# The mixer's input products of the second block from high and low parts, in three products instead of one four-byte product

## The reference

```python
def second_block(x, ...):
    for l in range(DEPTH):                                   # DEPTH = 2
        x = x + 0.5 * swiglu(rms_norm_2(x, norm_ffn1[l]), ffn1_in[l], ffn1_out[l])
        h = rms_norm_2(x, norm_mix[l])
        proj = h @ w_in[l]                                   # the mixer's input products
        p_rwkv, p_attn, p_gate = jnp.split(proj, [C_RWKV, C_RWKV + C_ATTN], axis=-1)
        o_a = rwkv7_mixer(p_rwkv, ...)                       # shift-mix, then a recurrent scan
        o_b = diff_attention(p_attn, ..., diff_lambda[l], ...)
        y = einsum(stack([o_a, o_b]), w_branch[l])
        x = x + sum(sigmoid(p_gate) * y) @ w_out[l]
        x = x + 0.5 * swiglu(rms_norm_2(x, norm_ffn2[l]), ffn2_in[l], ffn2_out[l])
```

## Time and profile before

| what | value |
|---|---|
| timed runs | 3978.73, 3982.89, 3984.99 us |
| the profiled execution | 3978.22 us, span 3976.5 us |
| busy share of the span | TensorE 86%, VectorE 39%, ScalarE 21%, GpSimd 15% |
| mean granted TensorE clock | 0.909 of full |
| second block | from 1953.7 us to the end |
| the mixer's input products | 2188.8 to 2282.1 us in layer 0, from 3195.2 us in layer 1 |

### The profile page before, as it was taken

How to read it: one execution, slowest core, us unless ns; L and a number is a source line. 1 busy time by engine, 2 the same in 40 slices (tenths; PEclk the granted TensorE clock), 3 DMA queues, 4 the chain that set the end, 5 groups by cost and what they waited for, 6 DMA issues and landing times.

```text
span 3976.5 us, 46296 instructions
## 1 busy us (share of the span) xinstructions
PE 3405.7 (86%) x18496; PEld 2349.6 (59%) x18496; DVE 1562.6 (39%) x2703; ACT 843.5 (21%) x1240; POOL 603.5 (15%) x556
## 2 busy tenths in 40 slices
PE   6878999993888799999199978787979997878799
PEld 3755334331566334333098658775978965868498
DVE  4433222224533222222454255543535425644354
ACT  1211111110130111111133232111324213111132
POOL 5402233331440233333000000000000000000000
PEclk8979999996878899999599988898999998889899
DMA  7646999995753899999554310003536422000442
GB/s 271 228 172 249 387 388 387 388 378 184 274 184 148 336 385 383 379 382 362 201 187 143 111 54 1 22 36 124 191 118 217 159 82 83 1 22 1 159 169 96
DMA packets 305420, 799.38 MB, mean 201 GB/s; under 512 B 57030, under 2 KB 155868, under 8 KB 251308
## 3 DMA queue, kind: packets, MB, share of 16 engines
q1 hardware_dynamic: 245804, 727.16, 48.4%
q0 software_dynamic: 58848, 67.05, 5.1%
q10 hardware_dynamic: 544, 2.10, 0.1%
HBM read 989.01 MB, written 53.48 MB: 262 GB/s over the span
## 4 chain that ended last, share of the span: by engine, by line
PE 41%; DVE 7%; ACT 1%; issue 1%; DMA 1%; SPq 0%; DVEq 0%
PE s_bank L1929 13%; PE s_bank L1967 6%; PE s_bank L1903 3%; PE s_bank L1916 3%; PE s_bank L2114 2%; PE s_bank L1994 2%; PE s_bank L2129 2%; PE s_bank L2225 2%; PE s_bank L2124 2%; PE s_bank L2235 1%; PE s_bank L2102 1%; DMA s_ringA<-in_ffn_in 1%; PE s_bank L2191 1%; PE s_bank L2025 0%; PE s_bank L2200 0%
## 5 line engine op out<-in xcount | busy, mean ns | idle before, releaser
L711 PE MATMUL f_bank<-f_ringA,f_arena 128*64 128x512 f32 x3072 | 689.8, 602 | 25.0 <-DMA f_ringA<-in_w_up,f_chosen 17.8
L711 PEld LDWEIGHTS f_bank<-f_ringA,f_arena 128*64 128x64 f32 x3072 | 216.5, 138 | 416.4 <-issue 415.2
L1929 PE MATMUL s_bank<-s_hT_high_parts,s_highA_parts 128*128 128x256 f32 x1408 | 402.1, 286 | 17.7 <-DVE s_hT_parts L2461 17.7
L1929 PE MATMUL s_bank<-s_hT_parts,s_highA_parts 128*128 128x256 f32 x1408 | 401.7, 285 | 0.0
L1929 PE MATMUL s_bank<-s_hT_high_parts,s_ringA_parts 128*128 128x256 f32 x1408 | 401.4, 285 | 0.0
L732 PE MATMUL f_bank<-f_ringB,f_arena 128*64 128x512 f32 x1536 | 346.1, 592 | 1.0 <-DVE f_arena L1475 1.0
L1012 ACT ACTIVATE f_arena<-f_bank 128x512 f32<-128x512 f32 (+1 forms) x362 | 202.0, 587 | 575.3 <-PE f_bank L692 174.1
L1467 DVE TENSOR_TENSOR f_arena<-f_arena,f_bank 128x256 f32<-128x256 f32 x96 | 58.6, 610 | 600.3 <-ACT f_arena L1090 600.3
L1929 PEld LDWEIGHTS s_bank<-s_hT_high_parts,s_highA_parts 128*128 128x128 f32 x1408 | 273.6, 194 | 20.4 <-issue 19.0
L1929 PEld LDWEIGHTS s_bank<-s_hT_parts,s_highA_parts 128*128 128x128 f32 x1408 | 273.6, 194 | 1.4
L1929 PEld LDWEIGHTS s_bank<-s_hT_high_parts,s_ringA_parts 128*128 128x128 f32 x1408 | 273.6, 194 | 0.0
(11 more groups left out here) (398 smaller groups left out, 5565.5 us busy)
## 6 DMA issues: line engine op xcount, KB each, us to landing
f_ringA<-in_w_gate SPq DMA_DIRECT2D x128, 1024.0 KB, 8.8
f_ringA<-in_w_up SPq DMA_DIRECT2D x128, 1024.0 KB, 11.6
f_ringB<-in_w_down SPq DMA_DIRECT2D x128, 1024.0 KB, 12.6
s_ringA<-in_ffn_in SPq DMA_DIRECT2D x88, 1024.0 KB, 7.6
f_ringA<-in_w_ada SPq DMA_DIRECT2D x48, 1024.0 KB, 8.6
s_arena<-in_ffn_out SPq DMA_DIRECT2D x44, 1024.0 KB, 6.1
s_ringA<-in_w_in SPq DMA_DIRECT2D x40, 1024.0 KB, 6.8
f_ringA<-in_w_in SPq DMA_DIRECT2D x28, 1024.0 KB, 10.3
```

Of the source, the lines that this page charges most:

```text
L711: last = mm(ps[j * CAP:(j + 1) * CAP, :].rearrange("p (h c) -> p h c", h=2), picked[:, b % 2, k, j * CAP:(j + 1) * CAP], gu[j][:, :, k, :] ...
L1929: last = mm(ps[:, t * S:(t + 1) * S], parts_of(wx[:, k, cs_]), parts_of(hx[:, k, :]), start=(k == 0 and x == 0), stop=(k == DT - 1 and x = ...
```

## The change

In the two layers of the second block the 168 plain products per layer become 504 products of parts. `hT` stays in full (the gates need it), its low part goes to a buffer of its own, `hT_low`. `mix_up(c)` on ScalarE rounds chunk c into `highA`, `mix_down(c)` on VectorE leaves the low part in the slot; chunk 0 is done inside the last step of the feed-forward in front, chunk c+2 after chunk c's banks have been taken. Chunk 6 has 384 columns per row of eight, the others 512. VectorE's wait for lambda's exponential moves behind `mix_down(4)`.

```diff
+        hT_low = parts_of.part("hT_low", arena, arena_at, 20480, 2048).rearrange("p (t s) -> p t s", s=S)
...
+        MIX = 7
+
+        def mix_chunk(c):
+
+            width = 512 if c < MIX - 1 else CRW - 1536
+            return [rows8(w)[:, :, 0:width] for w in (slotA(a_at + c), highA[:, (STEPS + c) % 2, :])]
...
                 for c in range(3):
-                    landed(a_at + c)
-                    w = rows8(slotA(a_at + c))
+                    pe.wait_ge(mix_low, c + 1)
+                    w, high = mix_chunk(c)
                     for m in range(MT):
                         ps = banks.claim(pe, ("at", c, m))
                         for k in range(DT):
-                            last = mm(ps[:, :], hT[:, k, m * P:(m + 1) * P], w[:, k, :],
-                                      start=(k == 0), stop=(k == DT - 1))
+                            if c == m == 0 and k % 2 == 0:
+                                pe.wait_ge(mix_split, k // 2 + 1)
+                            for x, (hx, wx) in enumerate(((hT_high, high), (hT_low, high), (hT_high, w))):
+                                last = mm(ps[:, :], parts_of(hx[:, k, m * P:(m + 1) * P]), parts_of(wx[:, k, :]),
+                                          start=(k == 0 and x == 0), stop=(k == DT - 1 and x == 2))
...
                 for g in range(8):
-                    c = a_in + g // 2
                     if g % 2 == 0:
-                        landed(c)
-                    w = rows8(slotA(c))
+                        pe.wait_ge(mix_low, 3 + g // 2 + 1)
+                    w, high = mix_chunk(3 + g // 2)
...
+                    for t in range(1 if g == 7 else 2):
+                        o = (2 * (g % 2) + t) * P
+                        for k in range(DT):
+                            for x, (wx, hx) in enumerate(((high, hT_high), (high, hT_low), (w, hT_high))):
+                                last = mm(ps[:, t * S:(t + 1) * S], parts_of(wx[:, k, o:o + P]), parts_of(hx[:, k, :]),
+                                          start=(k == 0 and x == 0), stop=(k == DT - 1 and x == 2))
...
+            def mix_up(c):
+
+                a_filled(act, a_at + c)
+                banks.read(act, ("u", 0, STEPS - 2 + c) if c < 2 else ("at", c - 2, 1) if c < 5 else ("rw", 2 * (c - 5) + 1))
+                w, high = mix_chunk(c)
+                f(parts_of(high), w, ACT.Copy).then_inc(mix_high, 1)
+
             def norm(k, at):
 
+                if k == 1:
+                    mix_up(0)
...
-                        last = f(hT[:, j, :], ps[:, t * S:(t + 1) * S], ACT.Copy, scale=cols[:, at + j:at + j + 1])
-                        if k != 1:
-                            last = f(parts_of(hT_high[:, j, :]), ps[:, t * S:(t + 1) * S], ACT.Copy,
-                                     scale=cols[:, at + j:at + j + 1])
+                        f(hT[:, j, :], ps[:, t * S:(t + 1) * S], ACT.Copy, scale=cols[:, at + j:at + j + 1])
+                        last = f(parts_of(hT_high[:, j, :]), ps[:, t * S:(t + 1) * S], ACT.Copy,
+                                 scale=cols[:, at + j:at + j + 1])
...
                 norm(1, r_mix)
+                mix_up(1)
                 for c in range(3):
                     for m in range(MT):
                         take(("at", c, m), at_tok[:, m, c * 512:(c + 1) * 512], lambda ps: ps[:, :])
+                    mix_up(c + 2)
...
+                    if g in (1, 3):
+                        mix_up(5 + g // 2)
...
-                    if k != 1:
-                        for b in range(4):
-                            banks.evacuated(dve, ("xT", k, b))
-                            two = slice(2 * b, 2 * b + 2)
-                            tt(parts_of(hT[:, two, :]), hT[:, two, :], parts_of.value(hT_high[:, two, :]),
-                               ALU.subtract).then_inc(hT_split, 1)
+                    for b in range(4):
+                        banks.evacuated(dve, ("xT", k, b))
+                        two = slice(2 * b, 2 * b + 2)
+                        tt(parts_of((hT_low if k == 1 else hT)[:, two, :]), hT[:, two, :], parts_of.value(hT_high[:, two, :]),
+                           ALU.subtract).then_inc(mix_split if k == 1 else hT_split, 1)
+                    if k == 1:
+                        mix_down(1)
...
+                def mix_down(c):
+
+                    w, high = mix_chunk(c)
+                    dve.wait_ge(mix_high, c + 1)
+                    tt(parts_of(w), w, parts_of.value(high), ALU.subtract).then_inc(mix_low, 1)
...
+                    if k == 0:
+                        mix_down(0)
...
-                dve.wait_ge(lam_exp, 1)
-                step(tt(lam[:, 4:5], lam[:, 3:4], lam[:, 2:3], ALU.subtract))
-                step(tt(lam[:, 4:5], lam[:, 4:5], lamc[:, 0:1], ALU.subtract))
-
+                mix_down(2)
                 for c in range(2):
                     for m in range(MT):
                         banks.evacuated(dve, ("at", c, m))
+                mix_down(3)
+                dve.wait_ge(lam_asked, 1)
...
                 variance(small[:, 0:32], small[:, 120:152], 1.0 / HD, 1e-6)
+                mix_down(4)
+                dve.wait_ge(lam_exp, 1)
+                step(tt(lam[:, 4:5], lam[:, 3:4], lam[:, 2:3], ALU.subtract))
+                step(tt(lam[:, 4:5], lam[:, 4:5], lamc[:, 0:1], ALU.subtract))
                 root(32)
...
+                    if g in (1, 3):
+                        mix_down(5 + g // 2)
```

More of the change, by code:

```diff
@@ L1642, in second_block @@
         lowB_ready, hT_split, hid_split = each["lowB_ready"], each["hT_split"], each["hid_split"]
+        mix_high, mix_low, mix_split = each["mix_high"], each["mix_low"], each["mix_split"]
         merged, dve_steps, arrived = each["merged"], each["dve_steps"], each["arrived"]
@@ L1993, in _ @@
                         for k in range(DT):
-                            last = mm(ps[:, :], hT[:, k, m * P:(m + 1) * P], w[:, k, :],
-                                      start=(k == 0), stop=(k == DT - 1))
+                            if c == m == 0 and k % 2 == 0:
[3 more added lines that the diff above has]
+                                          start=(k == 0 and x == 0), stop=(k == DT - 1 and x == 2))
                         banks.fill(last, ("at", c, m))
                 for g in range(8):
-                    c = a_in + g // 2
                     if g % 2 == 0:
-                        landed(c)
-                    w = rows8(slotA(c))
+                        pe.wait_ge(mix_low, 3 + g // 2 + 1)
+                    w, high = mix_chunk(3 + g // 2)
                     ps = banks.claim(pe, ("rw", g))
-                    o = (g % 2) * 2 * P
-                    banks.fill(hidden(ps, w[:, :, o:o + 2 * P], 1 if g == 7 else 2), ("rw", g))
+                    for t in range(1 if g == 7 else 2):
[4 more added lines that the diff above has]
+                                          start=(k == 0 and x == 0), stop=(k == DT - 1 and x == 2))
+                    banks.fill(last, ("rw", g))
                 pe.wait_ge(at_ready, 1)
```

10 lines of the change are left out of this document (5 added, 5 removed).

## The result

The changed kernel takes 3955.82 us (median of 4 runs, 3950.94 to 3960.59), the kernel before 3983.94 us (4 runs, 3978.73 to 3985.77). The ratio is 0.9931 with a 95% interval of 0.9914 to 0.9949: 28.1 us faster. The profiled execution took 3950.94 us, its span is 3949.0 where 3976.5 stood.

What follows compares the result with a forecast made beforehand. TensorE was taken to bound the changed stage. Per layer 17.3 saved on products, less 1.9 start and 1.6 clock, gives 13.8 us, 27.6 for two; 3980.8 - 27.6 = 3953.2, predicted 3953 us, range 3944 to 3966.

Steps and rivals of the forecast that it cites:

- The products: Mixer products of parts at 0.228 and 0.120 us, from feed-forward rows: 76.0 us for 93.25, 17.3 less per layer.
- The rival of one pass per product: Mixer products of parts cost 0.216 and 0.108 us, saving 23.3 us per layer; time 3941, chance 0.04.
- The start: Mixer's first product waits for hT_high and the first subtraction: 1.86 us lost per layer.
- The clock: Low clock after TensorE's longer idle gap before the mixer's products: 1.6 us per layer, bounds 0 and 2.2.
- Parts in time: Mixer chunks' roundings and subtractions cost nothing; rival, parts late: 5.7 us per layer, time 3965, chance 0.16.
- Chunk 0: Its subtraction on VectorE ends 0.25 us before VectorE takes the feed-forward's first output bank.
- chunk 5: Tightest mixer chunk: mix_down(5) ends at S + 22.3, TensorE wants it at S + 23.0; cover about 0.5 us.
- S: TensorE's start on the mixer's recurrent chunks, from which chunk 5's times are counted.
- a hand-over: 0.2 us taken off chunk 5's cover of 0.7 us, leaving about 0.5.
- The DMA's cover: Mixer chunk c+3, asked for at the end of chunk c, lands 4 us before ScalarE wants it.
- Given back: Rival: work behind the mixer not hanging on TensorE keeps its place; time up to 3981, chance 0.06.
- Slower: Rival: highA's two buffers do not overlap, 9.1 us chain at chunks 2 to 6; time 4043, chance 0.04.

Runs made afterwards that it cites:

- the two repetitions: The changed kernel unaltered, measured again twice as after_again and after_beside: 3957.02 and 3957.39 us, ratios to the kernel before 0.9936 and 0.9938.
- filler: Changed kernel plus 14 unused identity products between the mixer norm's transposes and first product: 3958.52 us, kernel before 3974.47.
- four_products: Changed kernel plus a fourth product, low part by low part, for each of the 168: 4006.35 us, kernel before 3978.93.
- after_again: The changed kernel unaltered, measured again: 3957.02 us (6 runs), kernel before 3981.26, ratio 0.9936.
- after_beside: The changed kernel unaltered, measured once more on the chip of another run: 3957.39 us (6 runs), kernel before 3979.86, ratio 0.9938.
- attn_only: Changed kernel with only the attention's products in parts, the recurrent branch's 120 per layer left plain: 3981.43 us, kernel before 3974.47.
- rec_only: Changed kernel with only the recurrent branch's products in parts, the attention's 48 per layer left plain: 3980.19 us, kernel before 3974.47.
- low0_late: Changed kernel with VectorE's subtraction of chunk 0 moved behind the feed-forward's four output banks: 3963.79 us, kernel before 3974.47.
- lam_first: Changed kernel with VectorE's wait for lambda and its two instructions moved in front of mix_down(4): 3952.87 us, kernel before 3978.93.
- one_buffer: Changed kernel with every mixer chunk rounded into the same half of highA instead of two: 4089.69 us, kernel before 3978.93.

## Why the prediction was right

I said 3953 us, 27.6 less; it is 3955.8, 28.1 less than the before measured beside it (in the two profiled executions 27.5 in the span). That the two differ by only 0.5 us is in part luck, since the two repetitions gave 24.2 and 22.5; the mechanism is confirmed by the terms. Layer 0 from first transpose to first score product, term by term:

| term | before | forecast | after |
|---|---|---|---|
| first transpose to first product | 4.94 | 6.80 | 6.80 |
| attention's products | 41.44 | 32.8 + 1.6 | 34.23 |
| recurrent products | 51.81 | 43.2 | 43.21 |
| last product to scores | 6.48 | 6.48 | 6.48 |
| sum | 104.7 | 90.9 | 90.7 |

- *The products*: 0.228 and 0.120 us held, also in filler and four_products. Counting passes gave the direction, but the rows were the better price, by 6 us per layer. four_products shows the difference by itself; why a product of parts takes 12 ns more than a quarter of a plain one stays open. The rival of one pass per product falls.
- *The start*: 1.86 us, exact. VectorE's first write is at 2186.48 and the first product 3.96 us later, where the second feed-forward's norm gave 3.97: the same instructions in the same order.
- *The clock*: 1.6 taken, 1.4 and 1.5 found, and filler shows the cause. But I had called 2.2 the upper bound, from two rows, and it isn't one. In the 16 mixers measured here with such a gap, 2.9 to 3.5 us (two each of after, after_again, after_beside, attn_only, rec_only, low0_late, lam_first and four_products; one_buffer, with its other waits, is left out), 13 lost 1.4 to 1.7 us and 3 lost 2.7 to 3.0 (after_again and after_beside in layer 0, low0_late in layer 1). In these three the clock never rose between the norm and the products. after_beside, layer 0:

```profile
2192.94:2198.97 6.03, 6.03 (x14) 4.76 (x15) 6.03 (x5) 0.86 (x1) 0.00 (x0) 0.50 0.00 0
2198.97:2228.66 29.69, 29.69 (x133) 24.57 (x132) 11.48 (x6) 10.03 (x7) 0.00 (x0) 1.00 0.41 142
```

  Here the products' first 6 us ran at 1.2 GHz, and half of that is lost. The Trainium skill (TensorE: Matmul & The Clock Gate, HAM oscillation) warns that a gap in front of products makes the next ones run cold and that half of the cold time is lost. The traces agree: all 16 mixers lost time so, which no row of before could show for a gap of this length.
- *Parts in time*: no wait, so the rival falls. Chunk 0 had 0.38 us (I said 0.25). The mis-sized term is chunk 5: I gave it 0.5 us, and it had 1.4. VectorE in the kernel after:

```profile
2241.93 4.42 DVE L2503 TENSOR_TENSOR s_ringA_parts<-s_ringA,s_highA_parts 128x4096 fp32r<-128x4096 f32 x1
2246.26 0.68 DVE L2584 TENSOR_TENSOR s_arena<-s_edge 128x512 f32<-128x512 f32 x1
```

  It began at S + 17.3 and ended at S + 21.7 (S is 2224.67), where I had 17.9 and 22.3: I added durations of a dozen instructions, and each starts some 0.08 us before the record in front ends (2241.93 + 4.42 is 2246.35, the next begins at 2246.26). The second error was to take a hand-over off as well. The DMA's cover, 4 us by my count, was 3.4 at chunks 3 and 4 (the second half of chunk 3 landed at 2210.90, its rounding began at 2214.32).
- *Given back*: the scores follow the last product by 6.48 us as before, and the scan is 476 us in both profiles, so in these two nothing was given back. It isn't closed, though: all 14 long scans lie among the 26 of changed kernels, and the kernel before has one profile, with two short ones. If its executions have the long scan less often, that would give back some of the 27.6 us, and the 24.2 and 22.5 of the repetitions leave room for it. Two scans can't show it.
- *Slower*: one_buffer has its mechanism and its price, 7.5 to 9.4 us per chunk against 9.1 reckoned, and 2.3 more for the clock that I hadn't put in. It also waits at six chunks, where I had counted five.

## What to carry to other kernels

Take the price of a new kind of product from the same kind elsewhere in the trace, not from the number of passes: here the pass count promised 25% and the rows gave 19%. Before work is moved under TensorE's stream, write down for each piece when it ends and when it is wanted; count starts of instructions, not sums of durations, and add to a new idle stretch of TensorE the low clock behind it (here 2.9 us of idle time were enough for it, 1.66 us were not). And compare stages of the profile, since a stage elsewhere may move by a good part of the effect, here up to 11 us in the two scans.

## What the runs showed of the hardware

Behind TensorE's idle stretches of 2.9 to 3.5 us the granted clock was low in the first products or fell within 0.8 us of their start, in all 16 mixers; it was 1.00 behind the 1.66 us of before. Products with no use in the gap kept it up (32.79 us for the 144 products, where 32.8 was expected).

The scan's two lengths are one late rise of the clock. In after and after_beside the instructions from the first score product up to there run alike, to within 1 us; windows on the same stretch in layer 0, after, then after_beside:

```profile
2349.00:2367.30 18.30, 8.08 (x34) 7.57 (x35) 13.47 (x19) 5.53 (x8) 0.00 (x0) 0.50 0.00 0
2367.30:2384.40 17.10, 11.38 (x65) 10.35 (x65) 13.13 (x29) 0.67 (x2) 0.00 (x0) 0.80 0.00 1
```

```profile
2353.00:2372.00 19.00, 8.13 (x34) 7.60 (x35) 14.13 (x22) 5.52 (x8) 0.00 (x0) 0.50 0.00 0
2372.00:2393.50 21.50, 18.01 (x63) 15.11 (x62) 13.71 (x29) 0.60 (x1) 0.00 (x0) 0.50 0.00 1
```

Both stretches come out of 18 to 19 us at 1.2 GHz in which TensorE is under half busy. In the one the clock rises at the first products of a dense row, and they take 11.4 us; in the other it stays at 0.50 to the end of the row, and nearly as many take 18.0. Behind it, one execution is about 5 us later, against its own first score product, than the other, to the end of the scan. Of the 28 scans in the profiles of this study, 14 are of the long kind, in kernels whose scan is word for word the same. The traces tell the two kinds apart earlier than that: in the 14 long scans the granted clock fell 70.0 to 71.8 us behind the first score product and stayed low for 44.4 us, in the 14 short ones it fell 72.0 to 73.1 us behind it and stayed low for 20.5 us. So the length goes with where in the work the clock falls. What sets that, and whether the change moves it, stays open: no experiment was made on it.
